# The values of a gated recurrence in seven block products in place of eight, in both layers of a two-block model

## What is computed

```python
for l in range(DEPTH):
    h = x @ w_in[l]
    (hg_q, hg_f, hg_i, hg_gate, mla_cq, mla_ckv, mla_kr, mla_gate,
     mem_q, mem_gate) = jnp.split(h, IN_OFFSETS, axis=-1)
    y_hg = _hgrn2_group(hg_q, hg_f, hg_i, lower_bounds[l], hgrn_out_norm[l])
    ...
    y = y @ w_out[l]
    x = _layernorm(DEEPNORM_ALPHA * x + y, ln_g[l], ln_b[l])
```

## Time and profile before

| | us |
|---|---|
| median of three runs | 1394.65 |
| lowest, highest | 1394.02, 1395.52 |
| the profiled execution | 1393.01 |
| its span, first to last instruction | 1391.2 |
| TensorE matmul busy in the span | 1270.6 (91%) |
| VectorE | 812.6 (58%) |
| GpSimd | 652.6 (47%) |
| ScalarE | 436.0 (31%) |

### The profile page before, as it was taken

One profiled execution on the slowest core, in us unless ns is written; L12 is line 12 of the kernel. 1 busy time (PEld: TensorE's weight loads), 2 busy tenths in 40 slices (PEclk: granted clock), 3 DMA queues, 4 the chain that ended last, 5 costly groups with the idle time before them and its releaser, 6 DMA issues.

```text
span 1391.2 us, 17185 instructions
## 1 busy us (share of the span) xinstructions
PE 1270.6 (91%) x6328; PEld 784.6 (56%) x6328; DVE 812.6 (58%) x1694; ACT 436.0 (31%) x1065; POOL 652.6 (47%) x647
## 2 busy tenths in 40 slices
PE   9999999999999999999999999988787877887786
PEld 8887686648887686549655565633333333333232
DVE  0776377441566287352357774869988654444445
ACT  1533344111334334222234443333323232222223
POOL 0556667431646667432204455445444545445550
PEclk9999999999999999999999999999998989999999
DMA  9544335546444344647449999999999999999995
GB/s 373 214 167 167 136 119 216 203 160 222 157 167 183 122 160 175 247 147 269 164 174 415 421 372 421 410 422 421 421 420 422 420 422 420 421 421 421 421 420 244
DMA packets 54061, 406.77 MB, mean 292 GB/s; under 512 B 6213, under 2 KB 8666, under 8 KB 11610
## 3 DMA queue, kind: packets, MB, share of 16 engines
q0 software_dynamic: 37184, 268.45, 46.6%
q1 hardware_dynamic: 15706, 136.18, 25.5%
q10 hardware_dynamic: 1088, 1.05, 0.4%
HBM read 403.53 MB, written 1.07 MB: 291 GB/s over the span
## 4 chain that ended last, share of the span: by engine, by line
PE 35%; DMA 20%; DVE 8%; ACT 2%; issue 1%; POOL 0%; DVEq 0%; ACTq 0%; POOLq 0%
PE bank L1181 13%; DMA kM<-in_peer_uv,vM 8%; PE pj L746 7%; PE pj L782 5%; PE pj L1044 4%; PE pj L761 3%; DMA qM<-in_peer_uv,vM 3%; DMA b<-in_peer_uv,vM 2%; DMA yT<-in_peer_uv,vM 2%; DMA more_rows<-in_peer_uv,vM 2%; DMA ring<-in_peer_uv,vM 2%; DVE ring L2001 1%; DVE kM L2001 1%; ACT rope L1417 1%; PE bank L706 0%
## 5 line engine op out<-in xcount | busy, mean ns | idle before, releaser
L746 PE MATMUL pj<-xT,ring 128*128 128x256 f32 (+1 forms) x1568 | 318.4, 363 | 0.9 <-ACT hv L1351 0.4
L746 PEld LDWEIGHTS pj<-xT,ring 128*128 128x128 f32 x1568 | 276.6, 190 | 36.5 <-issue 2.6
L642 POOL TENSOR_SCALAR more_rows<-more_rows,lbt 128x256 f32<-128x256 f32 x168 | 175.7, 1046 | 16.4
L681 POOL DMA_INDIRECT ring<-in_peer_uv,vM x100 | 114.1, 1141 | 123.8 <-PE bank L1181 110.3
L2001 DVE SCALAR_TENSOR_TENSOR ring<-ring,memT 128x1024 f32<-128x1024 f32 x101 | 122.2, 1225 | 76.8 <-DMA ring<-in_peer_uv,vM 72.6
L1415 ACT ACTIVATE rope<-vM 128x1 f32<-128x1 f32 (+2 forms) x112 | 22.6, 202 | 382.0 <-DVE ring L2001 146.8
L782 PE MATMUL pj<-ring,yT 128*128 128x512 f32 x320 | 140.8, 594 | 0.0
L640 POOL TENSOR_SCALAR mod_part<-more_rows,lbt 128x256 f32<-128x256 f32 x24 | 23.8, 991 | 246.0 <-issue 121.0
L643 POOL TENSOR_TENSOR mod_part<-mod_part,more_rows 128x256 f32<-128x256 f32 x168 | 127.1, 756 | 14.0
L1181 PE MATMUL bank<-ring,tri 128*128 128x512 f32 x212 | 103.1, 631 | 24.0 <-ACT tri L1423 20.2
L1181 PE MATMUL bank<-ring,causal 128*128 128x512 f32 x188 | 90.3, 625 | 11.0 <-ACT causal L1423 11.0
(11 more groups left out here) (399 smaller groups left out, 2093.0 us busy)
## 6 DMA issues: line engine op xcount, KB each, us to landing
ring<-in_units SPq DMA_DIRECT2D x42, 2048.0 KB, 9.5
more_rows<-in_w_ada SPq DMA_DIRECT2D x24, 1024.0 KB, 4.9
ring<-in_units SPq DMA_DIRECT2D x2, 1536.0 KB, 7.7
home<-in_units SPq DMA_DIRECT2D x1, 2048.0 KB, 14.3
ring<-in_peer_uv,vM POOLq DMA_INDIRECT x100, 26.7
memT<-in_mem SPq DMA_DIRECT2D x2, 512.0 KB, 5.4
ring<-in_units SPq DMA_DIRECT2D x1, 1024.0 KB, 9.2
xT<-in_x_turned SPq DMA_DIRECT2D x1, 1024.0 KB, 11.1
```

The source lines that it names most:

```text
L642: do(g.tensor_scalar(mod_w[:, c, :], mod_w[:, c, :], silu_c[:, c:c + 1], None, ALU.mult))
L681: pool.indirect_dma_start(row_slot[k], None, d["peer_uv_2"], bass.IndirectOffsetOnAxis(ap=expert[:, t, j:j + 1], axis=0))\
L746: ins = nc.tensor.matmul(pj[s][0:n, 2 * m + first:2 * m + stop], ring[:, slot, at:at + n], act[:, c, first:stop], start=(c == 0), stop=(c ...
```

## The change

The product of x with the 1024 value columns is cut into blocks: x into 2 x 2 (two halves of the positions, two halves of the inner dimension), the weights into 2 x 2 (two halves of the inner dimension, I0 and I1). In place of eight block products the kernel makes seven, J1 to J7, by the scheme of Strassen in Winograd's form. Each is four matmuls of 128x512. For this

- GpSimd makes four sums of blocks of x (128x512 each) ahead of piece 2 of each layer, in `home`, and four sums of weight blocks (128x2048 each) in place in `ring`, ahead of piece 4. The first of them needs both units, the second J3, the third J1, the fourth J2. The fourth, too, stands ahead of piece 4.
- I1 and I0 follow one another in the stream of units and lie in the ring together until J4, and MV takes I1's late place. J3 and J1 are made where I0a was, J5 and J2 where I0b was, J6 and J7 where MV was, J4 behind P5. J3, J1, J6 and J4 use `pj0`, the others `pj1`.
- ScalarE copies one product (JA) in place of the two units, and copies Q1 before level 6's exponentials, not after S4's. Its copy of MV moves behind HN1. VectorE adds up the blocks with seven additions from PSUM (JC, JU, JV, JW).

Core of the diff; the tasks of ScalarE and VectorE change as told above, and layer 1's list of TensorE as layer 0's:

```diff
-            P1 L05 Y1 LD AD I0a P2 LD L06 LD S4 S5 P3 I0b Y2 AD Y3 AD P4 MV Y4 L07 P5 G0a L08 LD Y5 LD AD G0b MQ LD
-            AD HO0 S6 HO1 HN0 L11 GEa AD P6 S7 GEb S8 HN1 L12 LD I1 Y6 L13 P7 P8 S9 L14 Y7 G1a G1b P9 Y8 AD L15 LD L16
+            P1 L05 Y1 LD AD J3 J1 P2 LD L06 LD S4 S5 P3 J5 J2 Y2 AD Y3 AD P4 J6 J7 Y4 L07 P5 J4 G0a L08 LD Y5 LD AD G0b MQ LD
+            AD HO0 S6 HO1 HN0 L11 GEa AD P6 S7 GEb S8 HN1 L12 LD MV Y6 L13 P7 P8 S9 L14 Y7 G1a G1b P9 Y8 AD L15 LD L16
...
+            def sums_of_blocks(l):
...
+                do(g.tensor_tensor(s1, x21, x22, ALU.add))
+                do(g.tensor_tensor(s2, s1, x11, ALU.subtract))
+                do(g.tensor_tensor(s3, x11, x21, ALU.subtract))
+                do(g.tensor_tensor(s4, x12, s2, ALU.subtract), "x_sums")
+
+            def sums_of_values(l, last):
+
+                w11, w12, w21, w22 = value_blocks(l)
+                if last:
+                    pool.wait_ge(sem("j_product2"), l + 1)
+                    do(g.tensor_tensor(w21, w21, w22, ALU.subtract), "j_weights4")
+                    return
+                for name in ("I1", "I0"):
+                    n = UNIT[l, name]
+                    pool.wait_ge(sem(f"ring_load{n % RING}"), ring_loads(n))
+                do(g.tensor_tensor(w12, w12, w11, ALU.subtract), "j_weights1")
+                pool.wait_ge(sem("j_product3"), l + 1)
+                do(g.tensor_tensor(w22, w22, w12, ALU.subtract), "j_weights2")
+                pool.wait_ge(sem("j_product1"), l + 1)
+                do(g.tensor_tensor(w11, w22, w11, ALU.subtract), "j_weights3")
+
             pool.wait_ge(sem("silu_c"), 1)
             for j in range(N_MOD_PIECES):
+                l, piece = j // (N_MOD_PIECES // DEPTH), j % (N_MOD_PIECES // DEPTH)
+                if piece == 2:
+                    sums_of_blocks(l)
+                if piece == 4:
+                    sums_of_values(l, False)
+                if piece == 4:
+                    sums_of_values(l, True)
                 pool.wait_ge(sem("mod_load"), 16 * (j + 1))
...
+            def values_product(l, task):
...
+                rows, w, dst = {3: (s4, w22, a1), 1: (x11, w11, a0), 5: (s1, w12, b0), 2: (x12, w21, b1),
+                                6: (s2, w22, a0), 7: (s3, w11, b1), 4: (x22, w21, a0)}[k]
+                for c in range(DC // 2):
+                    ins = nc.tensor.matmul(dst, rows[:, c, :], w[:, c, :], start=(c == 0), stop=(c == DC // 2 - 1))
```

More of the change, by code:

```diff
@@ L116, in unit_of @@
 def unit_of(task):
+    if task in ("J3", "J1"):
+        return {"J3": "I1", "J1": "I0"}[task]
     known = task[:2] in ONE_SLOT or output_unit(task[:2])
@@ L167, in big_uses @@
             turn = 0
+        elif name == "I1":
+            out[l, "J"] = tuple(uses)
+            uses = [uses[0] + 1, uses[1] + 1]
+            turn = 1
+        elif name == "I0":
+            pass
         elif name in ONE_SLOT or name == "C":
@@ L491, in up_weights, with value_blocks, x_blocks @@
                     w[:, UQ_W + 512:UQ_W + 1024])
+        def value_blocks(l):
+            return [ring[:, UNIT[l, name] % RING, :].rearrange("p (c n) -> p c n", c=DC)[:, half:half + DC // 2, :]
+                    for half in (0, DC // 2) for name in ("I0", "I1")]
+        def x_blocks():
+            return [xT[:, half:half + DC // 2, t * P:(t + 1) * P] for t in range(TT) for half in (0, DC // 2)]
         def ring_loads(n):
@@ L1707, in _ @@
                             do(v.tensor_tensor_scan(sums[:, n * P:(n + 1) * P], seg, seg, 0.0, ALU.add, ALU.bypass))
+                    elif task[0] == "J":
+                        c11, c12, c21, c22 = [hv[:, t, half * COLS:(half + 1) * COLS] for t in range(TT) for half in range(2)]
+                        if task == "JC":
+                            dve.wait_ge(sem("j_copied1"), l + 1)
+                            dve.wait_ge(sem("j_product2"), l + 1)
+                            do(v.tensor_tensor(c11, c22, pj[1][:, COLS:], ALU.add), "j_seen2")
+                        elif task == "JU":
+                            unit_done(dve, l, "I1")
+                            do(v.tensor_tensor(c21, c22, pj[0][:, 0:COLS], ALU.add), "j_seen6")
+                            do(v.tensor_tensor(c12, c21, pj[1][:, 0:COLS], ALU.add))
+                        elif task == "JV":
+                            dve.wait_ge(sem("j_product7"), l + 1)
+                            do(v.tensor_tensor(c22, c12, pj[1][:, COLS:], ALU.add))
+                            do(v.tensor_tensor(c21, c21, pj[1][:, COLS:], ALU.add), "pj_free1", BIG[l, "J"][1] + 1)
+                            do(v.tensor_tensor(c12, c12, pj[0][:, COLS:], ALU.add))
+                        else:
+                            unit_done(dve, l, "I0")
+                            do(v.tensor_tensor(c21, c21, pj[0][:, 0:COLS], ALU.add), "pj_free0", BIG[l, "J"][0] + 1)
+                            dve.sem_inc(sem("hv_ready"), 2)
                     elif task[:2] == "Da":
```

60 lines of the change are left out of this document (46 added, 14 removed).

## The result

The changed kernel takes 1448.5 us at the median of four runs (1447.8 to 1455.1), against 1395.1 for the kernel before: a ratio of 1.039 (95% interval 1.036 to 1.043). It is 53 us slower. The forecast was 1437 us, with 1432 to 1443 as its own spread and 1428 to 1450 with the rivals. The sign and the place of the loss were right. The loss was 11 us larger than forecast, so the time lies outside the forecast's own spread, and inside the wide range only by what the rivals had added to it.

What follows compares the result with a forecast made beforehand. Bound: TensorE and GpSimd as equal chains meeting at the fifth and eighth modulation products. Layer 0 adds 21.5 us, layer 1 20.9, together 42.4 on 1393.0: 1435.4, with the median 1.6 above: 1437 us, range 1428 to 1450.

Steps and rivals of the forecast that it cites:

- two chains of equal length: TensorE and GpSimd, between the fifth and eighth modulation products: shortening one gains nothing alone, lengthening one is paid in full.
- the second wait at the eighth product: TensorE waits again for GpSimd's piece 7 in layer 0: 59.0 us against 58.1, so 0.9 us.
- the clock of one half behind the stall: After TensorE's idle time at the fifth modulation product its granted clock is about half, costing 2.4 us.
- Y6's 1.2 us: Y6, right behind MV, waits for ScalarE to copy MV out: 1.2 us in each layer.
- It costs nothing more: J3 starts late behind ScalarE's copy of Q1, TensorE loses 2.1 us, covered by its wait at the fifth product.
- late load: Piece 3's weights are issued behind I0, so GpSimd starts piece 3 at 117.7, not 111.33: 6.4 us late.
- hidden load: Piece 4's load, in which GpSimd idled 5.0 us, runs behind the sums and is subtracted from GpSimd's added time.
- (a): Rival: VectorE stretches GpSimd's sums, 6.6 us more for the four, 2 x 6.6 added: 1450 us; 15%.
- (b): Rival: TensorE paces the fifth to eighth product, pieces 5 to 7 run faster, 3.3 us earlier a layer: 1430 us; 14%.
- (c): Rival: TensorE's clock stays low longer, losing 6 us after each stall, 2 x 2.7 more: 1442 us; 5%.
- (d): Rival: faster; with short sums TensorE never waits at the fifth product, saving 2.3 us a layer: 1390 us; 3%.
- (e): Rival: the stalls are absorbed somewhere behind, so no change in time; 1%.

Runs made afterwards that it cites:

- tiny_sums: The changed kernel with each of the four weight sums made over 16 of its 2048 columns, all waits kept: 1432.3 us (ratio 1.027).

## Why the prediction was right, and where it failed

**Right.** That two chains of equal length meet at the fifth product, that GpSimd's is lengthened there, that TensorE idles some 18 us (17.95 and 18.30), that the 3.5 us of removed matmuls are swallowed, the second wait at the eighth product (1.53), the clock of one half behind the stall, and Y6's 1.2 us. The sums, tested by themselves in the kernel before, put the product at 160.41, where that run's expectation had 160.4. TensorE's own path from the fifth to the eighth product took 58.0 us (59.54 less the wait of 1.53), for 58.1.

**The step that failed** is the sentence that the four sums' products "are no later: ... J2 is done at 146, before the fourth sum starts at 147". The margin was 1 us, and J2's time was taken from a timeline in which GpSimd ran only instructions of about 1 us and J3 ran at full clock. J3's lower clock (5.37 us for 3.60), which the prediction put at nothing ("It costs nothing more"), took 1.8 us, and J2 still was in time in layer 0 only because the sums were late too. In layer 1 VectorE was held for two whole sums, J2 came at 489.1, and the fourth sum waited 5.86 us: 5.2 us of that layer. A second, silent part of the same step was to add the terms (late load, sums, hidden load). In layer 0 they added only by luck, since J2 and the third sum ended within 0.6 us of each other (147.8 and 148.4). The runs show a maximum of two paths: the load alone changed is worth -4.1, with the fourth sum moved it is worth 12.1.

**The sizes.** Of the 13.0 us that are missing on the profiled execution (55.4 more span, 42.4 forecast), layer 0 has 2.7: the load landed after 11.4, not 10.0 us (piece 3 1.2 late, 0.9 at its end), the sums took 19.5, not 19.0, piece 4 0.5 more, and the stretch from the fifth product to Y6 another 0.7. Between Y6 and the third product of layer 1 lie 0.5 (24.24 late, then 24.78: 461.42 for 436.64). Layer 1 has 8.1: its Y6, at 594.18 for 540.38, is 53.8 late, 29.0 more, for 20.9. That is the 5.2 of J2, and the same small terms again. Behind that Y6 1.6 us were added; what made them I didn't follow.

**The rivals.** (a), 1450 us, came nearest in time, and had the right two engines, but the wrong one paying: a sum that met none of these instructions took 4.50 to 4.52 us (4.67 were forecast), and all four were stretched by 1.3 us in layer 0 and 0.7 in layer 1, while VectorE was held for 4 us at a time and passed it on to TensorE and, through J2, back to GpSimd. (b) fell: pieces 5 to 7 were no faster, and the eighth product waited for GpSimd. (c) was not needed: the clock's loss stayed under the cover of GpSimd's chain. (d) asked for sums of 0.2 us; tiny_sums had them and still took 1432, and with the wait for J2 gone as well 1414.8: (d) left out that wait and the late load. (e) fell: nothing behind took up the stalls.

## What to carry to other kernels

When work is put on GpSimd ahead of a piece that TensorE waits for, write down every product that the work itself waits for as a second path, and take the later of the two: a fix of one path alone is worth nothing or less, as the load's 7 us were. Price a long GpSimd instruction also by what it holds: nearly every VectorE instruction here with two SBUF inputs that started during a sum ended some 0.55 us behind it, and what waited for that one was late with it. Look for the places where two engines start within hundredths of a microsecond of each other. Here 0.02 us decided whether a layer paid 5 us, so a margin of 1 us behind such a place wasn't a margin.

## What of the hardware was not expected

A 128x512 instruction of VectorE with two SBUF inputs took up to 5.04 us in place of 0.69 beside GpSimd's sums of 128x2048, up to 1.80 beside quarters (128x512) and up to 2.72 beside halves (128x1024). The other way round, a GpSimd sum that met one lost only 0.3 to 0.6 us. Cut in quarters, the four sums of a layer took 23.8 us from first to last, where the whole ones took 19.5.
